# PEER expert layers: gates scattered into a zeroed routing matrix by one-element accumulating DMAs; U's low parts on DVE

## What is computed

```python
q = (h @ w_q).reshape(B, S, PEER_HEADS, 2, PEER_DK_HALF)
s = jnp.einsum('bshpd,hpkd->bshpk', q, keys)
s_top, i_top = lax.top_k(s, K)
cand = (s_top[..., 0, :, None] + s_top[..., 1, None, :]).reshape(B, S, PEER_HEADS, K * K)
cand_idx = (i_top[..., 0, :, None] * N_KEYS + i_top[..., 1, None, :]).reshape(B, S, PEER_HEADS, K * K)
best, pos = lax.top_k(cand, K)
idx = jnp.take_along_axis(cand_idx, pos, axis=-1)
gate = jax.nn.softmax(best, axis=-1)
act = jax.nn.gelu(jnp.einsum('thkd,td->thk', u_sel, hx), approximate=False)   # u_sel = u_tab[idx]
y = jnp.einsum('thk,thkd->td', gx * act, v_sel)                               # v_sel = v_tab[idx]
```

## Time and profile before

| | |
|---|---|
| three executions | 3307.57, 3310.97, 3313.2 us |
| the profiled execution, span from first to last instruction | 3305.3 us |
| instructions | 57051 |
| TensorE busy | 3189.0 us, 96% |
| DVE, ACT, POOL busy | 2607.8, 1161.1, 2052.8 us |
| moved by DMA | 856.31 MB, mean 259 GB/s |
| granted TensorE clock, mean | 0.988 |

### The profile page before, as it was taken

One profiled execution on the slowest core, in us unless ns is written; L12 is line 12 of the kernel. 1 busy time (PEld: TensorE's weight loads), 2 busy tenths in 40 slices (PEclk: granted clock), 3 DMA queues, 4 the chain that ended last, 5 costly groups with the idle time before them and its releaser, 6 DMA issues. The chain is left out here.

```text
span 3305.3 us, 57051 instructions
## 1 busy us (share of the span) xinstructions
PE 3189.0 (96%) x21428; PEld 2745.2 (83%) x21428; DVE 2607.8 (79%) x4810; ACT 1161.1 (35%) x1786; POOL 2052.8 (62%) x1304
## 2 busy tenths in 40 slices
PE   8998998899999999999999898999999999999998
PEld 3445887699999999888888777999999998888886
DVE  8583664589998886689899765899988866888997
ACT  0113544233334443333333423333344333333333
POOL 1122444377785655788888603777855568888884
PEclk9999998999999999999999999999999999999999
DMA  9750002377787887999999623777878889999995
GB/s 336 279 207 29 3 4 98 121 255 262 256 280 240 308 323 290 378 348 344 360 352 342 215 83 129 255 265 255 277 249 306 317 296 377 346 347 361 349 342 179
DMA packets 364075, 856.31 MB, mean 259 GB/s; under 512 B 32969, under 2 KB 201393, under 8 KB 355538
## 3 DMA queue, kind: packets, MB, share of 16 engines
q1 hardware_dynamic: 278610, 542.98, 47.3%
q0 software_dynamic: 85248, 310.42, 26.2%
HBM read 750.46 MB, written 102.81 MB: 258 GB/s over the span
## 5 line engine op out<-in xcount | busy, mean ns | idle before, releaser
L1804 PE MATMUL peer_acc<-peer_hhi,peer_uhi 128*128 128x384 f32 x2048 | 697.1, 340 | 8.4 <-POOL peer1same_ulo L2004 4.5
L1804 PE MATMUL peer_acc<-peer_hlo,peer_uhi 128*128 128x384 f32 x2048 | 686.2, 335 | 0.0
L2004 POOL TENSOR_TENSOR peer1same_ulo<-peer_u,peer_uhi 128x1024 fp32r<-128x1024 f32 x128 | 311.7, 2438 | 192.1 <-ACT peer_uhi L1884 190.7
L2004 POOL TENSOR_TENSOR peer0same_ulo<-peer_u,peer_uhi 128x1024 fp32r<-128x1024 f32 x128 | 311.7, 2438 | 191.9 <-ACT peer_uhi L1884 191.1
L1880 ACT ACTIVATE peer_gel<-peer_acc 128x384 f32<-128x384 f32 x256 | 125.7, 491 | 768.9 <-PE peer_acc L1804 768.9
L1804 PEld LDWEIGHTS peer_acc<-peer_hhi,peer_uhi 128*128 128x128 f32 x2048 | 386.3, 189 | 11.4 <-POOL peer1same_ulo L2004 5.8
L1804 PEld LDWEIGHTS peer_acc<-peer_hlo,peer_uhi 128*128 128x128 f32 x2048 | 386.2, 189 | 1.0 <-issue 0.5
L2035 POOL TENSOR_TENSOR peer0lsame_vlo<-peer0l_v,peer0l_vhi 128x1024 fp32r<-128x1024 f32 x128 | 310.3, 2424 | 85.6 <-ACT peer0l_vhi L1919 85.2
L2035 POOL TENSOR_TENSOR peer1lsame_vlo<-peer1l_v,peer1l_vhi 128x1024 fp32r<-128x1024 f32 x128 | 310.2, 2424 | 85.4 <-ACT peer1l_vhi L1919 84.7
L2067 DVE SCALAR_TENSOR_TENSOR peer_acc<-peer_row,peer_p_g,peer_acc 128x1024 f32<-128x1024 f32 x254 | 325.1, 1280 | 36.1 <-DMA peer_row<-in_pe_v,peer_idx 36.1
L1804 PE MATMUL peer_acc<-peer_hhi,peer0same_ulo 128*128 128x384 f32 x1024 | 343.7, 336 | 0.0
(11 more groups left out here) (453 smaller groups left out, 6892.7 us busy)
## 6 DMA issues: line engine op xcount, KB each, us to landing
peer_u<-in_pe_uT SPq DMA_DIRECT2D x256, 512.0 KB, 5.8
peer0l_v<-in_pe_v SPq DMA_DIRECT2D x128, 512.0 KB, 6.0
peer1l_v<-in_pe_v SPq DMA_DIRECT2D x128, 512.0 KB, 6.1
activations<-peer_gel SPq DMA_DIRECT2D x256, 192.0 KB, 6.1
rw_g<-in_ada POOLq DMA_DIRECT2D x60, 512.0 KB, 5.4
routing<-peer0m_wb SPq DMA_DIRECT2D x24, 1024.0 KB, 8.3
peer0l_wt<-routing SPq DMA_DIRECT2D x64, 384.0 KB, 7.5
peer0l_gl<-activations SPq DMA_DIRECT2D x128, 192.0 KB, 7.1
```

Source lines behind the costliest of these rows:

```text
L1804: mm = pe.matmul(ub[e % 2][:, 0:SD], a, h[:, k, 0:SD], start=(n == 0), stop=(n == 3 * KT - 1))
L2004: g.tensor_tensor(ulo[:, q].rearrange("p k e -> p (k e)"), u[:, q].rearrange("p k e -> p (k e)"), uhi[:, e % NH].bitcast(F32).rearrange("p ...
```

## The change

The gates are no longer spread by matmuls. Each layer has its own routing matrix in DRAM, laid out [expert, token] as one vector of 16384 x 384 cells.

- **Clearing.** During the RWKV scan POOL fills a tile with zeros and SP writes it over both matrices, 6 DMAs each (12 x 4.19 MB, rows of 2 KB), and waits for them at the end of the scan's block.
- **Scatter.** After each head DVE forms the cell number (expert x 384 + token) of each pick and normalises the head's gates (the exponential is per head now). POOL then issues 16 x 3 = 48 indirect DMAs per head, each with 128 one-element cells (one per partition), which add into DRAM; 384 per layer. Before a head's scatters it waits until all of the earlier heads' have landed. The U row fetches are threaded between them; those left over stand behind the last scatter.
- **U's low parts** and the query weights' (`low_u`, `low_query`) move from POOL to DVE, into `fill`.
- **Spacing.** Heads start at tiles 0, 10, 24, ... 94 (14 apart); no spread groups, transposes or stores of `wb`. From the last head on, DVE puts two dots behind each low part; dots left over come before the V stage.
- **V stage.** Gates come as one DMA of 192 KB a tile. All 128 rows are added in this stage; the first activations are loaded after the last is stored, the first gates after the last scatter has landed.

```diff
+            sp.wait_ge(zeros_made, 1)
+            for cells in routing:
+                to = cells.rearrange("(n a p q) -> n p a q", n=CLEARINGS, p=P, q=4 * P)
+                for n in range(CLEARINGS):
+                    sp.dma_start(to[n], zeros[:].unsqueeze(1).to_broadcast(list(to[n].shape))).then_inc(cleared, 16)
...
+            g.memset(zeros[:], 0.0).then_inc(zeros_made, 1)
...
-HEAD_TILES = 7
-BETWEEN_TILES = 8
-BLOCK_TILES = 16
+HEAD_AT = (0, 10, 24, 38, 52, 66, 80, 94)
+HEADS_END = 108
+LATE_DOTS = 2
+FILLS = 17
...
+                for q in range(NL):
+                    sp.wait_ge(gel_stored[q], 16 * (ET // NL))
+                for e in range(NU):
+                    load_act(e, e)
+                sp.wait_ge(scattered, scattered_by(HEADS))
+                for e in range(NU):
+                    load_gates(e, e)
...
-                    for q in range(G):
-                        mm = pe.matmul(hb[n % 2][:, q], hot_j[n % 2][:, q], hot_i[:, n % 2, q], start=True, stop=True)
-                    mm.then_inc(spread_done, 1)
...
+                def scatter(n, k, t):
+                    s = n * TOPK + k
+                    g.indirect_dma_start(w_cells, bass.IndirectOffsetOnAxis(ap=cells[:, t, s:s + 1], axis=0), gates[:, t, s:s + 1], None,
+                                         compute_op=ALU.add).then_inc(scattered, 16)
...
+                for n in range(HEADS):
+                    pool.wait_ge(gates_made, n + 1)
+                    for k in range(TOPK):
+                        while n_u < min(TOPK * (n + 1), HEAD_DOTS * n + NG + HEAD_DOTS * k // TOPK):
+                            fetch_u(n_u)
+                            n_u += 1
+                        if k == 0 and n > 0:
+                            pool.wait_ge(scattered, scattered_by(n))
+                        for t in range(DT):
+                            scatter(n, k, t)
+                while n_u < SLOTS:
+                    fetch_u(n_u)
+                    n_u += 1
...
                 def fill():
-                    if n_dots[0] < may_dot[0]:
+
+                    n, i = at
+                    at[1] += 1
+                    while n_low[0] < head_at[n] + 2 + (head_at[n + 1] - head_at[n]) * (i + 1) // FILLS:
+                        low_u(n_low[0])
+                        n_low[0] += 1
+                    if n + 1 < HEADS and i in (8, 12):
+                        low_query(n + 1, (i - 8) // 4)
+                    while n > 0 and n_dots[0] < HEAD_DOTS * (n - 1) + HEAD_DOTS * (i + 1) // FILLS:
                         dot(n_dots[0])
                         n_dots[0] += 1
...
+                for e in range(n_low[0], ET):
+                    low_u(e)
+                    for _ in range(LATE_DOTS):
+                        dot(n_dots[0])
+                        n_dots[0] += 1
+                while n_dots[0] < SLOTS:
+                    dot(n_dots[0])
+                    n_dots[0] += 1
```

More of the change, by code:

```diff
@@ L582, in spread, with phase_rwkv_scan @@
     return cols.unsqueeze(2).to_broadcast([P, cols.shape[1], n])
[L585 removed]
+def phase_rwkv_scan(nc, made, const, arena, rw, p, D, S, w_o, w_out, routing):
     with ExitStack() as ctx:
@@ L1965, in _ @@
                     take_v(e, 0, e)
+                act.wait_ge(dot_done, SLOTS)
+                a.activation(dots[:], dots[:], ACT.Gelu).then_inc(dots_gelu, 1)
                 with act.Fori(0, V_TURNS) as i:
@@ L2103, in _ @@
                     second = val[:, 1].unsqueeze(2).to_broadcast([P, TT, TOPK, TOPK])
-                    ch(v.tensor_tensor(cand[:], first, second, ALU.add))
+                    together([v.tensor_tensor(cand[:], first, second, ALU.add)])
                     flat = lambda x, t: x[:, t].rearrange("p a b -> p (a b)")
@@ L2152, in _ @@
-                dve.wait_ge(dots_gelu, 1)
-                ch(v.tensor_tensor(p_g[:], dots[:], gate_g[:], ALU.mult))
+                    v.tensor_scalar(idx[:, col], idx_f[:, GT], float(layer * ET * P), None, ALU.add).then_inc(idx_made, 1)
+                    if n == 0:
+                        dve.wait_ge(token_made, 1)
+                    ch.send(v.scalar_tensor_tensor(out=cells[:, :, col], in0=idx_f[:, 0:DT], scalar=float(SD), in1=token[:],
+                                                   op0=ALU.mult, op1=ALU.add))
@@ new lines, in _ @@
+                    dve.wait_ge(exp_made, n + 1)
+                    ch(v.tensor_reduce(total[:], gates[:, :, col], AX.X, ALU.add))
+                    ch(v.reciprocal(total[:], total[:]))
+                    v.tensor_tensor(gates[:, :, col], gates[:, :, col], spread(total[:], TOPK), ALU.mult).then_inc(gates_made, 1)
+                    assert at[1] == FILLS
+                for e in range(n_low[0], ET):
+                    low_u(e)
+                    for _ in range(LATE_DOTS):
+                        dot(n_dots[0])
+                        n_dots[0] += 1
@@ L2176, in _ @@
                         weigh(e + 2)
+                    if e == FIRST_ROWS:
+                        dve.wait_ge(dots_gelu, 1)
+                        ch(v.tensor_tensor(p_g[:], dots[:], gates[:, GT], ALU.mult))
                     while n_rows < rows_after(e):
@@ L2229, in hybrid_trunk @@
                hi=area("wohi", fixed.offset + 4 * KT * D)("w", [P, KT, D], F32R))
-    phase_rwkv_scan(nc, first, const, area("scan", rwa.offset), rw, pr, D, S, w_o, rw_w_o[0])
+    phase_rwkv_scan(nc, first, const, area("scan", rwa.offset), rw, pr, D, S, w_o, rw_w_o[0], routing)
     keep = area("kept", kept_at)
```

271 lines of the change are left out of this document (86 added, 185 removed).

## The result

The changed kernel takes **3942.62 us** (median of 4 runs, 3938.41 to 3953.94) beside 3309.3 of the kernel before on the same chip: ratio 1.1915, 95% interval 1.19 to 1.1929. It is slower by 633 us. The forecast had the sign and the engine right; its value of 3490, and its range up to 3800, fell short.

What follows compares the result with a forecast made beforehand. TensorE bounds the kernel before; after, POOL's issuing (71.9 + 12.6 + 3.5 = 88 us per head) delays V by 90 us a layer: 3305.3 + 180 = 3485 profiled, 3490 as median; range 3260 to 3800.

Steps and rivals of the forecast that it cites:

- POOL decides, and it issues without a pause: U stage: POOL needs 88 us per head against TensorE's 72.2, falls behind by 16 a head and runs without a pause.
- The step that failed: POOL in the U stage: each scatter issue priced like a row fetch, 1.24 us; bounds 0.94 and 2.18.
- the dearer case: Rival: adding makes a scatter issue take 2.18 us, 133 us per head, +450 a layer, 4210 us; chance 0.07.
- The port: U stage: POOL issues starting inside DVE's two-input operations wait for their end, 12.6 us per head; bounds 6.3 and 25.
- The landing wait: U stage: before each head's scatters POOL waits for all earlier ones to land, 3.5 us per head (2.8 to 6.1).
- First fetch at 60: U stage: head 0's gates are ready 60 us in; POOL then runs without a pause.
- The rule for the V stage's start: V starts at 125 + 8T, T being POOL's us per head (forecast 88); the change breaks even at T = 76.8.
- The tail, 65: From last scatter to V stage: 65 us, of which 54 for DVE's 40 dots and 7 low parts.
- The clearing, "hidden", 0: During the scan: zeroing 50.3 MB takes 138 us of DMA but is hidden; bounds 0 and +60.
- V stage, 0 (0 to +10): V stage: 16 more rows, 20 us of DVE, taken as no added time; bounds 0 and +10 a layer.
- The DMA engines as bound: Rival: one-element packets at 162 ns make the DMA engines bound the U stage, 104 us a head, 3745 us; chance 0.10.
- The faster rival: Rival: POOL keeps up in the U stage, T below 76.8; 3215 to 3290 us, value 3250; chance 0.20.

Runs made afterwards that it cites:

- third_scattered: Changed kernel with 16 scatters a head instead of 48, leaving out the gates of two of three token tiles: 3285.74 us, ratio 0.9925.
- rows_with_heads: Changed kernel with 16 dots a head instead of 10 (LATE_DOTS 1 instead of 2), so row fetches keep up with the heads: 3920.41 us, ratio 1.1847.

## Why the prediction was right or wrong

- **POOL decides, and it issues without a pause: right.** The chain and POOL's row of waits say it, and third_scattered shows it by taking two thirds of the scatters away: 657 us less.
- **The step that failed: "A scatter reads 128 indices as a fetch does, so 1.24 is my value".** It measured 1.86 (1.56 + 0.30). The price of an indirect DMA's issue follows what is done with the data: 0.94 to 1.0 for a fetch, 0.97 for a scatter that overwrites, 1.56 for one that adds; half the width takes only 0.13 off. 48 x 0.62 = 30 us a head, 238 a layer, 476 in all. The bounds of the text, 0.94 and 2.18, held it; taking the value at the nearest row, and leaving the dearer case at 0.07 as an extreme of 4210 with nothing between, did not. Between 1.24 and 2.18 lay all of 3490 to 4210, and nothing in the trace spoke for the lower end.
- **The port: right in kind, but its 12.6 a head was too high.** The mean lies 0.12 above the median: 6 us over 48 scatters, 7 with the fetches (mean 1080, median 1007), an estimate of the port's cost that comes near the lower bound of 6.3. A likely reason, not tried by itself, is that DVE waited for rows much of the time (438.1 us in the second U stage), so that fewer of its operations met an issue. Where they meet, it shows (POOL, then DVE, of the kernel after):

```profile
2884.80 3.76 POOL L1951 DMA_INDIRECT routing<-peer_gates,peer_cells  x1 [0.46 <-DMA routing<-peer_gates,peer_cells]
```

```profile
2884.60 1.20 DVE L2014 TENSOR_TENSOR peer1same_ulo<-peer_u,peer_uhi 128x1024 fp32r<-128x1024 f32 x1
2885.72 1.22 DVE L2020 TENSOR_TENSOR peer1aover_wlo<-peer1a_wq,peer1aover_whi 128x1024 fp32r<-128x1024 f32 x1
```

  The issue began inside two two-input operations that follow each other (2884.60 to 2886.94) and took its own 1.56 behind them. The Trainium skill, SBUF — State Buffer, "Who interferes with whom", lets two SBUF inputs hold up only a GpSimd instruction that reads SBUF; a scatter's issue reads its 128 cell numbers, and this row has it held.
- **The landing wait, 3.5 a head: wrong, and small.** 5.1 us in all of the run. The text took a fetch's landing of 4.0 to 7.3 for it; a scatter that the chain of the kernel after waits for, issued at 2771.24, had landed 3.06 us later, of which its issue is 1.56, so that the one fetch before the next head's scatters nearly covered the rest.
- **Ten fetches a head: a small miscount.** Of the 128 fetches 41 stand behind the last scatter, so 87 are issued in eight heads, 10.9 a head: about 1 us a head more.
- **First fetch at 60: right** (63.6). The rule for the V stage's start, 125 + 8T, gives 1007 with the measured T of 110.2; measured 1032.
- **The tail, 65: 86.** The text priced it by DVE's 40 dots and 7 low parts, and let the rows come in time after the first. DVE waited 33.2 us of the stretch for rows, which landed in 12.4 us (median) while U tiles, V tiles and rows filled the DMA engines (0.93, then 1.03); that their fullness is what delayed the rows is likely, not tried by itself. It makes 21 a layer more. rows_with_heads shows that hardly any of it (5.6 us) belongs to the landing and the gates' loads.
- **The clearing, "hidden", 0: +43** alone, +40 in the kernel after, inside its bound of 60 by luck, since it came by another way than the bound's. w_o was not late behind it on the queue: its loads went out when the scan was done (550.8 instead of 509.6), 150 us after SP had issued the last of the clearing. The text looked for who waits for a transfer. None did; TensorE's stream stood still in pieces, and its clock fell.
- **V stage, 0 (0 to +10): right** (+5.1 and +2.7).
- **Rivals.** The DMA engines as bound fell: the scatters landed in time; POOL waited 5.1 us for them in all. The price of a cell was less than either value of the text (90 and 162 ns): in rows_with_heads from 3320 to 3360, nearly all scatters, queue 0 moved 3137 packets in 21.4% of 16 engines' time, an estimate of 44 ns of one engine, or 2.7 over all. The Trainium skill, DMA: Bandwidth & Descriptors, "Measured (HBM→SBUF, 128 partitions, SWDGE, issued from GpSimd)", gives about 10.5 ns a packet, and by it the rival fell too. The outcome agrees; the figure is for reads into SBUF, and the trace's own is lower. The faster rival needed T below 76.8; only the plain write comes near that on POOL (48 x (1.12 + 0.30) + 14 = 82), and it brought a bound of its own, the stores. Dearer issue was the right mechanism at two thirds of its size (0.62 more instead of 0.94); that it comes from a second set of descriptors, as the text supposed, no run shows.

Of the 455 us between 3485 and 3940.5, the head's 110.2 in place of 88 makes 16 x 22.2 = 355 (the 476, less some 120 by which port and landing were too high, with the fetches a little too low), the tail 42, the clearing 40, the first fetch 7, the V stages 8: 452. With what the terms measured: clearing and scan +40, two U stages of 63.6 + 8 x 110.2 + 86.3 against 739 (+292.5 each), V stages +8: 633 of 635.2. The agreement is no test, since the terms come from the same trace.

Three things stay open: by what the DMA engines stand still under plain one-element writes every 1.27 us, whether late instruction packets are what slows the scan beside the clearing, and what the low parts on DVE cost or bring by themselves, which was not tried apart from the rest (third_scattered shows only that they fit).

## What to carry to other kernels

An engine that issues indirect DMAs is a resource to budget like TensorE: count the issues, multiply by a price measured for that very form (read, overwrite, accumulate), and compare with the stage, before counting what the change takes off the busy engine. Where that price is not in the trace and the sum crosses the break-even inside its bounds, forecast between the bounds, not at the nearest row. A large transfer that nobody waits for is still not free when it fills all DMA engines (43 us here for 50 MB): issued in pieces of 1 MB, one at a time, the same transfer cost nothing.

## What the runs showed of the hardware

- The issue of an indirect DMA with 128 indices by POOL took 0.93 to 1.01 us for a fetch of 4 KB rows, 0.97 for an overwriting scatter of one-element cells, 1.56 for an accumulating one and 1.42 for that over 64 partitions, each with 0.30 before the next.
- An accumulating scatter of 128 cells made 144 packets (80 with 64 cells), a plain one 32.
- Plain scatters of 128 one-element cells issued every 1.27 us held up other stores to DRAM, one for 35 us, with the DMA engines moving nearly nothing in 18 of 40 slices of 0.75 us; spaced at 2.0 us, or accumulating at 1.86, they did not.
- With the DMA engines full (share 1.04), TensorE's stream of small matmuls ran at 915 in 50 us instead of 1378, stood still in pieces of up to 3.6 us with no cause shown, and 14 instruction packets passed in 115 us instead of 21. At a share of 0.58 nothing was lost.
